# New step orders in the mixers and other operations at the stage ends, in an fp32 model of two blocks on one core

## The reference

```
first block, 2 layers, x: (256, 1024), six modulation vectors a layer = silu(c) @ w_ada + b_ada
  x += gate1 * rmsnorm(mixed(rmsnorm(x) * (1 + scale1) + shift1) @ w_mix_out)      stages m0, m1
       mixed: four branches (differential attention, latent attention with rotary positions,
       short gated convolution, 31-tap convolution with layernorm), each projected and gated
  x += gate2 * rmsnorm((silu(conv3(a)) * b) @ w_down), a, b = h @ w_up              stages f0, f1
second block, 4 layers
  x += 0.5 * swiglu(rmsnorm(x))                                                     ha0 .. ha3
  x += mixer(rmsnorm(x)): HGRN2 (layers 0, 3), mLSTM (1), window attention (2)      mx0 .. mx3
  x += 0.5 * swiglu(rmsnorm(x))                                                     hb0 .. hb3
  x += sigmoid(rmsnorm(x) @ w_ple_gate) * (p @ w_ple_proj)                          pl0 .. pl3
```

## Time and profile before

| | us |
|---|---|
| median of 3 runs (3653.0 to 3654.23) | 3654.07 |
| the profiled execution | 3641.96 |
| its span | 3639.9 |
| PE busy, DVE busy, ACT busy | 3291.6, 2496.5, 1758.8 |
| stage m0 | about 40 to 431 |
| m0's end to f0's matmuls at full pace | 431 to 456 |
| m1 | 672 to 1038 |
| mx0, mx1, mx2, mx3 | 1454 to 1662, 2069 to 2235, 2655 to 2780, 3190 to 3412 |

### The profile page before, as it was taken

The page is one execution under the profiler, slowest core; times in us unless marked ns, Lnnn a source line. Parts: engine busy times, 40 slices in busy tenths (PEclk is TensorE's granted clock), DMA queues, the critical chain, the costliest instruction groups (busy, mean ns, idle before and its releaser), DMA issues.

```text
span 3639.9 us, 64372 instructions
## 1 busy us (share of the span) xinstructions
PE 3291.6 (90%) x27058; PEld 3178.2 (87%) x27058; DVE 2496.5 (69%) x3768; ACT 1758.8 (48%) x2641; POOL 3.0 (0%) x6
## 2 busy tenths in 40 slices
PE   6788899887989999869999997999989999985898
PEld 6778899876989999759999987999968999985898
DVE  8877689886666766756676566666666666686656
ACT  4445444454544445555454445454455454464544
POOL 0000000000000000000000000000000000000000
PEclk9889999998999999979999999999989999997999
DMA  8444488443546565415656534655623655641453
GB/s 303 123 136 166 163 297 300 143 128 111 169 145 209 174 187 182 136 47 182 186 164 185 167 116 136 186 180 171 187 95 127 185 178 174 186 145 53 148 186 116
DMA packets 163920, 598.06 MB, mean 164 GB/s; under 512 B 18192, under 2 KB 18224, under 8 KB 163376
## 3 DMA queue, kind: packets, MB, share of 16 engines
q1 hardware_dynamic: 163632, 593.94, 51.1%
HBM read 592.82 MB, written 1.05 MB: 163 GB/s over the span
## 4 chain that ended last, share of the span: by engine, by line
PE 70%; DVE 21%; ACT 6%; issue 2%; DMA 1%; SPq 0%; DVEq 0%; ACTq 0%
PE ps L449 22%; PE ps L450 22%; PE ps L451 22%; DVE wlo L413 6%; DVE fa L1462 2%; ACT whi L401 2%; DVE hl L1666 1%; PE ps L622 1%; DVE land L506 1%; DVE tmps L530 0%; ACT L522 0%; DVE tmps L528 0%; DVE tmps L1804 0%; PE ps L712 0%; DMA land<-w_ada 0%
## 5 line engine op out<-in xcount | busy, mean ns | idle before, releaser
L449 PE MATMUL ps<-hh,whi 128*128 128x256 f32 (+1 forms) x5472 | 1561.4, 285 | 80.7 <-DVE hl L1666 32.8
L450 PE MATMUL ps<-hl,whi 128*128 128x256 f32 (+1 forms) x5472 | 1550.1, 283 | 0.0
L451 PE MATMUL ps<-hh,wlo 128*128 128x256 f32 (+1 forms) x5472 | 1545.1, 282 | 0.0
L413 DVE TENSOR_TENSOR wlo<-land,whi 128x1024 fp32r<-128x1024 f32 (+1 forms) x1032 | 1218.8, 1216 | 271.1 <-ACT whi L401 270.2
L449 PEld LDWEIGHTS ps<-hh,whi 128*128 128x128 f32 (+1 forms) x5472 | 1048.9, 192 | 93.3 <-issue 65.2
L401 ACT ACTIVATE whi<-land 128x1024 fp32r<-128x1024 f32 (+1 forms) x1032 | 1028.9, 1044 | 174.6 <-PE ps L451 161.5
L450 PEld LDWEIGHTS ps<-hl,whi 128*128 128x128 f32 (+1 forms) x5472 | 1048.9, 192 | 0.9
L451 PEld LDWEIGHTS ps<-hh,wlo 128*128 128x128 f32 (+1 forms) x5472 | 1048.0, 192 | 0.0
L449 PE MATMUL ps<-ra,whi 128*128 128x256 f32 (+1 forms) x2416 | 691.3, 286 | 29.6 <-DVE ra L1372 12.7
L451 PE MATMUL ps<-ra,wlo 128*128 128x256 f32 (+1 forms) x2416 | 688.4, 285 | 0.0
L450 PE MATMUL ps<-ra,whi 128*128 128x256 f32 (+1 forms) x2416 | 687.6, 285 | 0.0
(11 more groups left out here) (411 smaller groups left out, 2437.4 us busy)
## 6 DMA issues: line engine op xcount, KB each, us to landing
land<-w_gu SPq DMA_DIRECT2D x352, 512.0 KB, 3.6
land<-w_dn SPq DMA_DIRECT2D x176, 512.0 KB, 3.6
land<-w_in SPq DMA_DIRECT2D x136, 512.0 KB, 3.6
land<-w_ada SPq DMA_DIRECT2D x96, 512.0 KB, 3.7
land<-w_up SPq DMA_DIRECT2D x88, 512.0 KB, 4.2
land<-hg_in SPq DMA_DIRECT2D x64, 512.0 KB, 3.6
land<-w_down SPq DMA_DIRECT2D x44, 512.0 KB, 4.4
land<-ple_gate SPq DMA_DIRECT2D x32, 512.0 KB, 3.6
```

Source lines behind the costliest of these rows:

```text
L413: dve.tensor_tensor(w.lo, g.slot(n), w.hi.bitcast(F32), ALU.subtract).then_inc(*D_("w_lo", n))
L449: pe.matmul(out, w.hi, x.hi, start=first, stop=False, skip_group_check=skip)
L450: pe.matmul(out, w.hi, x.lo, start=False, stop=False, skip_group_check=skip)
L451: return pe.matmul(out, w.lo, x.hi, start=False, stop=last, skip_group_check=skip)
```

## The change

1. The planners are replaced by written orders (`MIX_ORDER`, `HGRN_ORDER`, `MLSTM_ORDER`, `SWA_ORDER`). Steps are cut finer: the read of a projection's result is a step of its own ("q_out", "f_out", "v_out", "gate_out", "qk_out", "merge0" to "merge3"), norms are cut in "norm" and "apply", the layernorm of a branch in "cf_sum", "cf_mean", "cf_square", "cf_norm", "cf_apply", "cf_silu".
2. Causal masks are added by TensorE: a 128 x 128 product of the identity and the mask goes on top of the scores in PSUM, two for each map. VectorE's addition goes; maxima and exponentials read PSUM, whose bank is free after the exponentials.
3. The rotary matmuls alternate over banks 3 and 4.
4. Stage ends: VectorE adds the squares of y's first three banks, so TensorE sums 8 passes in place of 16; ScalarE writes y times gate into SBUF (three quarters of it ahead of the logarithm), and VectorE's update is one multiplication and one addition of 512 columns for each quarter; Ln is taken from the sum in PSUM with scale and bias, VectorE's variance comes after it; `warm_tensor` issues 6 matmuls (12 passes) behind y's sum and 4 behind x's, whose result nobody reads.
5. `lead_tensor` interleaves the first two projections of f0, m1 and f1 chunk by chunk (`mix_tensor` calls it for m1's, with one projection for m0; so does a feed-forward stage of the second block).
6. The columns 88 to 96 of w_ada are spread over the loads of f1 so that they end 22 tiles before its last, and `gate_gain_vector` is called earlier in each stage.

The core of the diff (the cut pieces of the other steps are the same kind of edit as HGRN's "q"):

```diff
+def lead_tensor(g, pe, projections, x, ready):
+
+    D_, W = g.m.done, g.m.when
+    parts = []
+    for name, j, bank, freed in projections:
+        for i, half in enumerate(halves(j)):
+            n = take_tensor(g, pe, name, half)
+            if i == 0:
+                pe.wait_ge(*W(*g.banks.use(bank, *freed)))
+            parts.append((n, i, g.ps[bank][:, i * T:(i + 1) * T]))
+    for k in range(8):
+        pe.wait_ge(*W(*ready[k]))
+        for n, i, out in parts:
+            mm = mm3(pe, out, g.weights(n)[:, k * 128:(k + 1) * 128], x.chunk(k), k + i == 0, k == 7, skip=True)
+            if k == 7:
+                mm.then_inc(*D_("tile", n))
...
+def rough_scalar(g, act, key, sums, y):
+
+    D_, W = g.m.done, g.m.when
+    act.wait_ge(*W(*sums))
+    act.activation(y, g.ps[MISC][:, 0:T], ACT.Ln, bias=g.C("eps", 0, 1), scale=1.0 / D).then_inc(*D_("var_ln", *key))
+    act.wait_ge(*W("var_ln", *key))
+    act.activation(y, y, ACT.Exp, scale=-0.5).then_inc(*D_("rough", *key))
...
 def squares_tensor(g, pe, st):
     D_, W = g.m.done, g.m.when
     sq, ps = squares_buffer(g, st), g.ps[MISC]
-    pe.wait_ge(*W(*g.banks.use(MISC, "var", st)))
+    pe.wait_ge(*W(*g.banks.use(MISC, "newton", st, 0)))
     for p in range(4):
         pe.wait_ge(*W("square", st, p))
         for c in range(2):
             mm = pe.matmul(ps[:, 0:T], g.C("ones", 0, 128), xk(sq, 2 * p + c), start=p + c == 0, stop=p == 3 and c == 1)
     mm.then_inc(*D_("sumsq", st))
+    if st != "m0":
+        warm_tensor(g, pe, 4)
+
+
+def warm_tensor(g, pe, n):
+
+    pe.wait_ge(*g.m.when(*g.banks.freed[6]))
+    for _ in range(n):
+        pe.matmul(g.ps[6][:, 0:T], g.C("ones", 0, 128), g.C("rst", 0, T), start=True, stop=True)
...
-    rsqrt_scalar(g, act, (st,), g.t(8)[:, 0:T], g.small[:, 0:T])
+    rough_scalar(g, act, (st,), ("sumsq", st), g.t(8)[:, 0:T])
...
-    dve.wait_ge(*W("sumsq", st))
+    dve.wait_ge(*W("var_ln", st))
     dve.tensor_scalar(v, g.ps[MISC][:, 0:T], 1.0 / D, 1e-6, ALU.mult, ALU.add).then_inc(*D_("var", st))
...
+def ygated_scalar(g, act, st, p):
+
+    D_, W = g.m.done, g.m.when
+    B = g.small[:, 568:576]
+    act.wait_ge(*W("gate_gain", st))
+    for k in halves(p):
+        u = act.activation(xk(g.t(p), k % 2), xk(g.ps[p], k % 2), ACT.Copy, scale=B[:, k:k + 1])
+    u.then_inc(*D_("y_gated", st, p))
+
+
+def ysquare_vector(g, dve, st):
+
+    D_, W = g.m.done, g.m.when
+    sq = g.fa1[:, 2048:4096]
+    for p in (1, 2):
+        dve.wait_ge(*W("ysquare", st, p))
+        if p == 2:
+            dve.wait_ge(*W("ysquares", st, 1))
+        dve.tensor_tensor(sq[:, quarter(0)], sq[:, quarter(0)], sq[:, quarter(p)], ALU.add).then_inc(*D_("ysquares", st, p))
+
+
+def ysquare_tensor(g, pe, st):
+    D_, W = g.m.done, g.m.when
+    ps, sq = g.ps[MISC], g.fa1[:, 2048:4096]
+    pe.wait_ge(*W(*g.banks.use(MISC, "newton", "y", st, 0)))
+    for p, event in ((0, ("ysquares", st, 2)), (3, ("ysquare", st, 3))):
+        pe.wait_ge(*W(*event))
+        for c in range(2):
+            mm = pe.matmul(ps[:, 0:T], g.C("ones", 0, 128), xk(sq, 2 * p + c), start=p + c == 0, stop=p + c == 4)
+    mm.then_inc(*D_("ysum", st))
+    warm_tensor(g, pe, 6)
...
 def normed_scalar(g, act, st):
...
     act.preload_act_table_set(NORM_TABLE)
     for p in range(4):
         ysquare_scalar(g, act, st, p)
-    rsqrt_scalar(g, act, ("y", st), g.t(8)[:, 0:T], g.small[:, 0:T])
-
-
-def normed_vector(g, dve, st):
+        if p < 2 and st[0] == "f":
+            ygated_scalar(g, act, st, p)
+    for p in range(2 if st[0] == "f" else 0, 3):
+        ygated_scalar(g, act, st, p)
+    rough_scalar(g, act, ("y", st), ("ysum", st), g.t(8)[:, 0:T])
+    ygated_scalar(g, act, st, 3)
...
+def normed_vector(g, dve, st):
+    D_, W = g.m.done, g.m.when
+    v, r = g.small[:, 0:T], g.small[:, T:2 * T]
+    ysquare_vector(g, dve, st)
+    dve.wait_ge(*W("var_ln", "y", st))
     dve.tensor_scalar(v, g.ps[MISC][:, 0:T], 1.0 / D, 1e-6, ALU.mult, ALU.add).then_inc(*D_("var", "y", st))
     rsqrt_vector(g, dve, ("y", st), r, v, g.t(8)[:, 0:T], g.t(8)[:, T:2 * T])
     dve.wait_ge(*W("factor", "y", st))
...
+def added_vector(g, dve, st, p):
+    D_, W = g.m.done, g.m.when
+    s = g.x[:, quarter(p)]
+    dve.wait_ge(*W("y_scaled", st, p))
+    dve.tensor_tensor(s, s, g.t(p), ALU.add).then_inc(*D_("x", AFTER[st], p))
...
-        t, B = g.t(p), g.small[:, 568:576]
-        dve.tensor_tensor(v2(t), v2(g.ps[p][:, :]), bc2(g.small[:, T:2 * T]), ALU.mult).then_inc(*D_("y_scaled", st, p))
-        dve.wait_ge(*W("y_scaled", st, p))
-        for k in halves(p):
-            add = dve.scalar_tensor_tensor(xk(g.x, k), xk(t, k % 2), B[:, k:k + 1], xk(g.x, k), ALU.mult, ALU.add)
-        add.then_inc(*D_("x", nx, p))
+        t = g.t(p)
+        dve.wait_ge(*W("y_gated", st, p))
+        dve.tensor_tensor(v2(t), v2(t), bc2(g.small[:, T:2 * T]), ALU.mult).then_inc(*D_("y_scaled", st, p))
+        if p:
+            added_vector(g, dve, st, p - 1)
+        if p == 3:
+            added_vector(g, dve, st, 3)
...
-    ready = chunks("h", st)
+    lead = 2 if st in FIRST else 1
+    lead_tensor(g, pe, [(up, up0 + j, 4 + j, ("up_read", st, j)) for j in range(lead)], g.h, chunks("h", st))
+    if st not in FIRST:
+        norm2_tensor(g, pe, st)
     for p in range(NF // 2):
         for j in halves(p):
-            proj_tensor(g, pe, up, up0 + j, 4 + j % 3, ("up_read", st, j), g.h, ready)
-            ready = None
-            if j == 0 and st not in FIRST:
-                norm2_tensor(g, pe, st)
+            if j >= lead:
+                proj_tensor(g, pe, up, up0 + j, 4 + j % 3, ("up_read", st, j), g.h)
         if p:
...
+MIX_ORDER = """
+    norm:0 cf:0 cf:1 lam:0 conv:0 conv:1 cf:2 cf:3 qk:0 conv:2 conv:3 conv:4 scu:0 qk:1 conv:5 conv:6 scu:1 conv:7
+    qk:2 qk:3 conv:8 mla:0 conv:9 mla:1 tables:0 conv:10 v:0 v:1 conv:11 conv:12 tables:1 da_scores:0 conv:13
+    conv:14 da_combine:0 conv:15 mc:0 da_scores:1 conv:16 mla_square:0 da_combine:1 da_turn:0 da_scores:2 mla_norm:0
+    conv:17 da_values:0 conv:18 da_combine:2 da_turn:1 da_scores:3 mla_apply:0 da_combine:3 mla_square:1 scu:2
+    da_values:1 da_turn:2 scu:3 da_values:2 da_turn:3 uq:0 ya_square:0 mla_norm:1 sc_conv:0 conv:19 sc_conv:1
+    da_values:3 scb:0 sc_conv:2 sc_conv:3 ya_square:1 scb:1 gate2:0 gate2:1 wo2:0 merge2:0 wo2:1 mla_apply:1
+    ya_norm:0 merge2:1 wo2:2 gate2:2 merge2:2 gate2:3 wo2:3 uq:1 ya_apply:0 merge2:3 uq:2 ya_norm:1 rope:0 rope:1
+    ya_apply:1 rope:2 uq:3 rope:3 rope:4 kr_all:0 ukv:0 ukv:1 ukv:2 cf_sum:0 mv:0 ukv:3 mv:1 mla_scores:0 gate1:0
+    mla_scale:0 cf_mean:0 mla_scores:1 mla_turn:0 mla_scale:1 mla_scores:2 gate1:1 mla_turn:1 mla_scale:2
+    mla_values:0 mla_scores:3 cf_square:0 gate1:2 mla_values:1 cf_norm:0 mla_turn:2 mla_scores:4 cf_apply:0
...
-                pe.matmul(g.ps[b][:, 0:128], q[p0:p1, a:a + 128], k[p0:p1, a:a + 128], start=True, stop=True)
-                pe.matmul(g.ps[b][:, 128:384], q[p0:p1, a + 128:a + 256], k[p0:p1, a:a + 256], start=True,
-                          stop=True).then_inc(*D_("scores", st, kind, i, m))
+                for tb, end in ((0, 128), (1, 384)):
+                    pe.matmul(g.ps[b][:, tb * 128:end], q[p0:p1, a + tb * 128:a + tb * 128 + 128],
+                              k[p0:p1, a:a + tb * 128 + 128], start=True, stop=True)
+                    mm = pe.matmul(g.ps[b][:, end - 128:end], g.causal[:, 0:128], g.causal[:, 128:256], start=False,
+                                   stop=True, skip_group_check=True)
+                mm.then_inc(*D_("scores", st, kind, i, m))
...
-            pe.wait_ge(*W(*g.banks.use(MISC, "rot_sin", st, i)))
+            pe.wait_ge(*W(*g.banks.use(3 + i % 2, "rot_sin", st, i)))
             for c in range(2 if i < 4 else 1):
-                mm = pe.matmul(g.ps[MISC][0:96, c * T:(c + 1) * T], g.C("rot", 0, 96, 0, 96), xk(src, c), start=True,
+                mm = pe.matmul(g.ps[3 + i % 2][0:96, c * T:(c + 1) * T], g.C("rot", 0, 96, 0, 96), xk(src, c), start=True,
...
-    act.activation(S[:, 0:128], S[:, 0:128], ACT.Exp, bias=nm[:, 0:1], scale=scale, accum_out=sm[:, 0:1])
-    act.activation(S[:, 128:384], S[:, 128:384], ACT.Exp, bias=nm[:, 1:2], scale=scale, accum_out=sm[:, 1:2]).then_inc(
+    act.activation(S[:, 0:128], ps[:, 0:128], ACT.Exp, bias=nm[:, 0:1], scale=scale, accum_out=sm[:, 0:1])
+    act.activation(S[:, 128:384], ps[:, 128:384], ACT.Exp, bias=nm[:, 1:2], scale=scale, accum_out=sm[:, 1:2]).then_inc(
...
-    dve.tensor_tensor(S, ps[:, 0:384], g.C("mask3", 0, 384), ALU.add).then_inc(*D_("masked", *key))
-    dve.wait_ge(*W("masked", *key))
-    dve.tensor_reduce(mx[:, 0:1], S[:, 0:128], AX, ALU.max)
-    dve.tensor_reduce(mx[:, 1:2], S[:, 128:384], AX, ALU.max).then_inc(*S_("vector_step"))
+    dve.tensor_reduce(mx[:, 0:1], ps[:, 0:128], AX, ALU.max)
+    dve.tensor_reduce(mx[:, 1:2], ps[:, 128:384], AX, ALU.max).then_inc(*S_("vector_step"))
...
+HGRN_ORDER = """
```

(24 more changed lines are left out.)

554 lines of the change are left out of this document (245 added, 309 removed).

## The result

| | before | after |
|---|---|---|
| median of 4 runs each, side by side | 3654.15 us | 3465.95 us (3463.23 to 3468.48) |
| profiled execution, its span | 3641.96, 3639.9 | 3468.48, 3466.7 |
| PE, DVE, ACT busy | 3291.6, 2496.5, 1758.8 | 3254.7, 2475.9, 1762.6 |

The sign and the largest term were right. Three terms were off by a factor of 1.6 or more, and they partly cancelled.

The account below looks back on a forecast made before the run. The prediction took the mixers to be bound by waits within strict engine orders, 400 us open; 69 + 44 + 22 (mLSTM and window attention) + 18 = 153 off 3642 gave 3489, as a median 3501, range 3420 to 3600.

Parts of the forecast that it names:

- m0 and m1: First block's two mixer stages: new orders, two rotary banks and mask matmuls save 36 and 33 us, together 69.
- no wait of the rotary matmuls over 1 us: Sign of being right in m1: with two alternating banks, 11.0 us of rotary waits fall to 1.
- HGRN: Second block's mixers mx0 and mx3: the new order saves 22 us each, 44 together.
- covers about 6 + 7 + 3.8/2 = 15 us: In mx0, moving one finish, prepare and two gate tiles covers 15 us of waits; the clock's share adds 9.
- Window attention: Mixer mx2: exponentials of a head move ahead of the next scores, saving 12 of 41 us open.
- The gated ends: Ends of m0, f0, m1 and f1: 5.0 us saved at three and 3.5 at f1's, 18 together.
- Whether that counts hangs on the clock ... I take 5.0: Gated ends: 2.4 us saved each at half clock, 7.5 if fillers keep the clock up; 5.0 taken for three ends.
- Two tiles begun together ... TensorE no longer trails DVE: First projections after a gated end: a chunk feeds 12 matmuls, 1.41 us, against 0.80 for DVE to make one.
- Nothing gained: Second block's shorter factor (0.46 us, 16 stages) is hidden by up tiles: 0, or 7 us if that cover is missing.
- The waits move: Rival, chance 0.12: the next waits replace those removed; mixers save 30 instead of 135 us, giving 3606.
- Slower: banks kept longer: Rival, chance 0.07: projection and score banks held longer stop TensorE, costing 119 us with nothing recovered in mixers, giving 3755.
- More than forecast: Rival, chance 0.07: the orders recover over half of the 400 us open in the mixers, giving 3418.

Follow-up runs that it names:

- y4: The kernel after with the steps of all four mixers in the order of the kernel before: 3641.51 us, ratio to before 0.9961.
- y3: The kernel after with the causal mask added by VectorE into SBUF instead of by matmul, new orders kept: 3482.51 us.
- z1: The kernel after with all rotary matmuls on one bank and the second half of the HGRN stages in the old order: 3505.16 us.
- w1: The kernel after with the steps of window attention alone in the old order: 3500.40 us.
- x1: The kernel after with all four gated stage ends and the second block's factor put back as before, new orders kept: 3474.78 us.
- x4: The kernel after without the 12 and 8 filler passes of each gated end: 3468.58 us.
- z2: The kernel after with one tile starting f0, f1, m1, 28 and 20 filler passes, and m0's and m1's gated copies ahead of the last square: 3450.35 us.
- y2: The kernel after with 28 filler passes behind the first sum and 20 behind the second, for 12 and 8: 3466.43 us.
- x3: The kernel after with VectorE splitting the third and fourth feed-forward tiles' weights before reading tile 0, two tiles still in step: 3468.54 us.

## Why the prediction was right, and where not

**m0 and m1: right, for a mixed sum of reasons.** -37.8 and -29.7 (this with an end) for -36 and -38. The orders alone give 30 and 24 (y4), the mask by matmul about 9 and 3 (y3), the second rotary bank 3 and 5 (z1). These do not add up (42 for 37.8 in m0), since what the mask and the bank are worth depends on the order: with the old orders all of them together bring m0 6.6 us. The rotary waits did not fall from 11.0 to 1 but to 7.0 in m1: the longer part is for ScalarE's write of the operand, which no bank helps; the "no wait of the rotary matmuls over 1 us" that I named as a sign of being right is refuted. I had also charged 2.5 us a layer for the mask matmuls and counted VectorE's 9 us as already in the chains; y3 says that net of this the change is worth 11 us over both layers. m1's stretch came out at 336.5 us, within the 325 to 340 that I had named, with 15.1 us idle where I left 19. My "they are shorter than 0.118 us each" for the mask matmuls was wrong (last section).

**HGRN: mechanism right, size off, -70.5 for -44.** The failed step is "covers about 6 + 7 + 3.8/2 = 15 us" with 2 given back. In mx0 idle time fell by 23 us, from 52.4 to 29.1: I counted the long waits that an obvious move removes and let the other level waits stand, but these shrank too, all seven from 25.5 us (17.5 in the earlier trace rows and 8.0 in three more for another tile) to 16.2. Putting back the order of the second half alone costs 12 of the 35 us (z1). The stage length that I named as a sign, 180 to 192 us for mx0, was missed for this reason: it came out at 173.7. The clock's share was near: PE busy fell by 11.0 us for the same 1771 matmuls, for 9 forecast.

**Window attention: -24.3 for -12.** I took 12 of the 41 us open, 22.5 of them clock, without a working of its own. The whole stage, before and after:

```profile
2465.60:2784.20 318.60, 298.58 (x2177) 279.06 (x2175) 192.69 (x308) 153.53 (x279) 0.00 (x0) 0.93 0.45 141
2355.10:2649.40 294.30, 285.94 (x2176) 271.18 (x2174) 191.92 (x308) 152.34 (x279) 0.00 (x0) 0.98 0.44 153
```

Idle time fell by 11.7 us, from 20.0 to 8.4, which is the 12. TensorE's busy time for the same work fell by 12.6 us with the clock, and for that the sum had nothing. w1 and y4 show that this second part is not even fixed in the old order.

**mLSTM: -7.1 for -10**, within its bound.

**The gated ends: -18 forecast, 1.4 in f1's end and nothing in the three stretches with the other ends (x1); the step that failed most.** Four terms of it:
- "Whether that counts hangs on the clock ... I take 5.0": up to the first projection each end got about the 2.4 of the half-clock case (17.2 for 19.8, 16.6 for 19.1, f1 7.4 for 10.2). The fillers saved nothing (x4), as the 3.35 and 2.50 us of idle time behind them were enough for the fall. I named the remaining 2.5 us and took a value between the cases; the lower one was right. z2, whose three stretches are 14 us shorter than x1's, shows that most of the 18 was there to be had, with gaps closed and one tile.
- "Two tiles begun together ... TensorE no longer trails DVE": the chunks cost no wait now, but VectorE's next split stands behind the read of tile 0, and that read is late by 4.6 us. m0's end gains 2.6 us at the first projection and keeps 0.9 at the fourth group, and loses 2.3 more to the second wait behind it; with one tile it keeps 2.9. I costed the step where it starts and not what is queued behind it on the other engine.
- "DVE adds three of the squares beforehand, so the first sum has 8 passes, 1.8 us less": in f0 and f1 TensorE waits 0.98 us for that addition, where the old sum could start on the first square. T stands 1.26 us behind the last projection matmul for 0.12, so f0's end as a whole gains 1.4 us and not the 2.5 that its row from T on shows.
- The gated copies, costed at nothing with "the copies lie before the first sum is ready, three quarters of them": in m0 and m1 they don't. ScalarE's timeline in after:

```profile
392.54 0.60 ACT L742 ACTIVATE fa<-ps 128x512 f32<-128x512 f32 x1 [1.64 <-PE ps L453]
393.04 2.30 ACT L751 ACTIVATE tmps<-ps,small 128x256 f32<-128x256 f32 x6
395.18 0.52 ACT L549 ACTIVATE tmps<-ps,con 128x256 f32<-128x256 f32 x1
```

The six copies stand behind the last square and the Ln behind them, at 395.18, while the sum's last pass began at 393.94. z2 moves them ahead and its Ln starts 0.4 us sooner behind T. No table load stands between Copy and Ln, as forecast.

**"Nothing gained" in the second block: 3.8 us gained** in the three pl stages, of the 7 that I had named for the case that the cover is missing.

**The signs.** Half-clock stretches as many as before were to show me wrong. For the kernel as a whole they grew fewer (granted clock 0.948 before, 0.966 after, in the profiles), but at the ends they did not: every end of after still has half clock, and there the forecast was wrong. The 8 passes of the first sum and 14 to 18 us from T to the first projection came as named (17.2 in m0's end).

**The rivals.** "The waits move" is out by the result: idle time fell by 27 us in m1 and 23 in mx0. "Slower: banks kept longer" is out too: after's lists for m1, mx0 and mx1 have no projection waiting over 0.2 us for the read of a bank, and the wait of the scores (4.9 us in m1) stands in y3 without the kept bank. "More than forecast" (3418) was closer than its chance of 0.07 suggests: the truth lies 35 us below my value and 48 above it.

**The 12 us between profile and median.** I added before's 12 us to the forecast; after has -2.5. The granted clock of each execution bears on it: of the 38 of before beside the experiments, those with spans up to 3642.3 us had 0.946 to 0.951 and those of 3650 us and more had 0.941 to 0.945. So the difference goes with the clock, and before's profile (span 3639.9, clock 0.948) is of the shorter kind. In which stage it lies is not shown, as those executions have no trace; mx2, 318.6 in before's profile and 332.6 in y4's, is the stage that the traces point to. Of the 35 us by which I missed, 20.5 are in the sum (3489 for 3468.5) and 14.5 in this offset.

## What to carry to other kernels

When one tile of an in-order pipeline is begun together with another, look at what the other engine has queued behind the read of the first tile: it moves back by most of a tile (4.6 of 5.65 us here). Fillers that leave a gap of 2.5 us were worth nothing here; those that close it were worth 2.3 us at every stage end with two sums. Check the granted clock behind the gap, not the number of fillers. And where a stretch's granted clock is well under 1, price what a better order gives back in clock beside what it gives back in idle time (12.6 beside 11.7 us in window attention, 11.0 beside 23 in HGRN), and expect the old time itself to vary from run to run.

## What the hardware did that I had not expected

The granted clock was 0.58 behind an idle stretch of 2.50 us, much as the 0.57 behind 4.23 us (after, x4), and stayed at 1.00 where throwaway passes filled the gap (y2). But 2.50 us did not always lower it: in x3 the same projection ran at 1.00, behind a sum that had run at 0.50 over its first 5.4 us. With the same waits to 0.1 us, the same loop ran at 0.84 or 0.67 in two traces, 14 us of 134 (w1, y4). And an accumulating 128 x 128 mask matmul has a price of its own on TensorE. The 64 of them in after (durations in ns, minimum, median and maximum):

```profile
L1114 PE MATMUL ps<-causal x64: 305/328/474, 119.2 to 875.5; 128*128 128x128 f32 x64
```

From its start to the next matmul's start there are mostly 0.14 to 0.26 us at full clock where no wait follows (0.26 at 712.14 in m1) and 0.27 to 0.40 at half clock, against 0.118 us for a projection matmul with twice the columns. The 32 of a layer make some 8 us (8.1 in m1), where I bounded them by 0 to 3.8; part of that is the scores matmul ahead of each, which in the latent heads starts only 0.03 us earlier. The mask by matmul pays all the same (y3).
